# Five load buffers for the first mixer's weight blocks, loads ahead of the modulation chunks, query weights loaded late

## The reference

```python
sh1, sc1, g1, sh2, sc2, g2 = [m[:, None, :] for m in ada(c, ada_w[i], ada_b[i])]
h_l = rmsnorm(x, norm1_g[i]) * (1 + sc1) + sh1
p_lat = h_lat @ w_in
p_ctx = h_ctx @ w_in
q = (rmsnorm(cq, q_norm_g) @ w_uq).reshape(B, T, MLA_HEADS, QK_HEAD_DIM)
kv = (rmsnorm(ckv, kv_norm_g) @ w_ukv).reshape(B, T, MLA_HEADS, QK_NOPE_DIM + V_HEAD_DIM)
```

## Time and profile before

| | |
|---|---|
| median of 3 runs | 1814.38 us (1810.35 to 1815.94) |
| profiled execution | 1805.72 us |
| its span | 1803.9 us |
| mean granted clock of TensorE | 0.962 |
| TensorE busy | 1657.5 us, 92% |
| VectorE, ScalarE, GpSimd busy | 755.1, 435.7, 119.7 us |
| moved by DMA | 586.61 MB, mean 325 GB/s |
| first mixer's blocks 0 to 17 | 38.5 to 113.5 us |

### The profile page before, as it was taken

How to read it: one execution, slowest core, us unless ns; L and a number is a source line. 1 busy time by engine, 2 the same in 40 slices (tenths; PEclk the granted TensorE clock), 3 DMA queues, 4 the chain that set the end, 5 groups by cost and what they waited for, 6 DMA issues and landing times.

```text
span 1803.9 us, 21857 instructions
## 1 busy us (share of the span) xinstructions
PE 1657.5 (92%) x8294; PEld 993.8 (55%) x8294; DVE 755.1 (42%) x1187; ACT 435.7 (24%) x643; POOL 119.7 (7%) x151
## 2 busy tenths in 40 slices
PE   5899899999889999999999999999968897899776
PEld 2763588888678888876433433344423342344222
DVE  5566578787368787654211221222201120112022
ACT  3434554443354444353000000000000000000001
POOL 1752010000410000020000000000000000000000
PEclk8998999999999999999999999999988999899888
DMA  9623559885449887607999999999999999999995
GB/s 353 233 99 117 183 189 340 312 299 192 171 159 330 314 306 270 245 24 302 375 419 421 421 421 421 421 421 422 421 422 421 421 421 421 421 412 421 422 421 204
DMA packets 100430, 586.61 MB, mean 325 GB/s; under 512 B 12048, under 2 KB 13328, under 8 KB 44976
## 3 DMA queue, kind: packets, MB, share of 16 engines
q1 hardware_dynamic: 100336, 585.35, 82.1%
HBM read 584.26 MB, written 1.05 MB: 324 GB/s over the span
## 4 chain that ended last, share of the span: by engine, by line
PE 78%; DMA 11%; DVE 5%; SPq 4%; issue 1%; ACT 1%; DVEq 0%; ACTq 0%
PE psum L1244 23%; PE psum L1260 11%; PE psum L912 4%; PE psum L913 4%; PE psum L914 4%; SPq L421 3%; PE psum L1220 3%; DMA mraw<-gu_dram 3%; PE psum L1029 3%; PE psum L1273 3%; PE psum L933 2%; PE psum L935 2%; PE psum L934 2%; DMA araw<-ada_dram 2%; PE psum L729 2%; PE psum L731 2%
## 5 line engine op out<-in xcount | busy, mean ns | idle before, releaser
L1244 PE MATMUL psum<-mraw,xsat 128*64 128x512 f32 (+2 forms) x1640 | 411.3, 647 | 55.2 <-DMA mraw<-gu_dram 40.9
L1244 PEld LDWEIGHTS psum<-mraw,xsat 128*64 128x64 f32 (+2 forms) x1640 | 135.6, 144 | 305.7 <-issue 304.6
L1260 PE MATMUL psum<-mraw,xsat 128*64 128x512 f32 (+2 forms) x856 | 205.9, 621 | 17.1 <-DMA mraw<-dn_dram 9.9
L912 PE MATMUL psum<-wh,ah 128*128 128x512 f32 x352 | 139.6, 397 | 2.6 <-DVE al L1917 1.8
L1260 PEld LDWEIGHTS psum<-mraw,xsat 128*64 128x64 f32 (+2 forms) x856 | 68.2, 140 | 133.2 <-issue 131.1
L913 PE MATMUL psum<-wl,ah 128*128 128x512 f32 x352 | 137.3, 390 | 0.0
L914 PE MATMUL psum<-wh,al 128*128 128x512 f32 x352 | 137.3, 390 | 0.0
L1803 POOL TENSOR_TENSOR wl<-raw,wh 128x256 fp32r<-128x256 f32 x132 | 108.6, 858 | 396.1 <-DVE work L1944 219.9
L2455 DVE TENSOR_TENSOR oacc<-psum,oacc 128x512 f32<-128x512 f32 x60 | 38.6, 686 | 220.3 <-PE psum L1273 220.3
L1244 PE MATMUL psum<-mlast,xsat 128*64 128x512 f32 (+2 forms) x408 | 118.2, 627 | 0.0
L1965 DVE TENSOR_TENSOR wl<-raw,wh 128x1024 fp32r<-128x1024 f32 x88 | 103.6, 1219 | 33.1 <-ACT wh L1525 33.1
(11 more groups left out here) (374 smaller groups left out, 2423.7 us busy)
## 6 DMA issues: line engine op xcount, KB each, us to landing
mraw<-gu_dram SPq DMA_DIRECT2D x205, 1024.0 KB, 19.2
mraw<-dn_dram SPq DMA_DIRECT2D x107, 1024.0 KB, 25.6
araw<-ada_dram SPq DMA_DIRECT2D x128, 512.0 KB, 4.9
mlast<-gu_dram SPq DMA_DIRECT2D x51, 1024.0 KB, 20.2
raw<-ffa_dram SPq DMA_DIRECT2D x44, 1024.0 KB, 5.1
raw<-ffb_dram SPq DMA_DIRECT2D x44, 512.0 KB, 5.3
mlast<-dn_dram SPq DMA_DIRECT2D x21, 1024.0 KB, 24.2
raw<-blk_dram SPq DMA_DIRECT2D x34, 512.0 KB, 4.8
```

Source lines behind the costliest of these rows:

```text
L912: mm(o, ah3[:, j, tok], wh[:, w], start=(j == 0), stop=False)
L1244: last = mm(ps[4 + n][a * w:(a + 1) * w, :], xs[:, k * P + a * w:k * P + (a + 1) * w], slots[slot][:, i * 2 * D + n * 512:i * 2 * D + (n + ...
L1260: last = mm(ps[n][a * w:(a + 1) * w, :], at[:, k * P + a * w:k * P + (a + 1) * w], slots[slot][:, i * D + n * 512:i * D + (n + 1) * 512], ...
```

## The change

It moves nothing on TensorE, VectorE, ScalarE and GpSimd; the order of their instructions stays. It changes three things.

1. Blocks 3 to 17 rotate over five buffers (`NFIRST_RAW`), the fourth and fifth at columns 3072 and 4096 of `raw`, where the query weights were. Load b waits for cast and subtraction b - 5 for b below 18. The semaphores of the two added buffers are reused from the pairs (`s_afirst[1:3]`), so `RAW_LOADED` gives the count that cast b waits for.
2. In the queue blocks 3 and 4 come ahead of chunks 16 and 17, behind a wait for the third pair product, since the pair lies in these columns. Blocks 7 to 10 come in one piece, and from then on block 9 + n comes ahead of chunk 16 + n, where before chunk 16 + n came ahead of block 6 + n.
3. The query weights are loaded behind block 17, after subtraction 14; `q_product` waits for them by a semaphore of their own (`s_uq`). `uk` and `cone` wait for the fourth pair product only.

The diff, without its hunks of line numbers:

```diff
...
 B_2 = B_Q2
 B_OUT2 = 48
 NB = 56
-NRAW = 3
+NRAW, NFIRST_RAW = 3, 5
 PIECE = 256
 SPLIT = [b % 6 for b in range(B_O)] + [0, 1, 4, 5, 2, 3, 4, 5] * 2
 SPLIT_BEFORE = [max([k + 1 for k in range(b) if SPLIT[k] == SPLIT[b]], default=0) for b in range(B_2)]
-RAW = [(5120 if b >= B_O + NRAW else 0) + (b % NRAW) * D for b in range(B_2)]
+RAW_SLOT = [b % NFIRST_RAW if b < B_O else (b - B_O) % NRAW for b in range(B_2)]
+RAW_LOADED = [16 * (RAW_SLOT[:b + 1].count(RAW_SLOT[b]) + (RAW_SLOT[b] >= NRAW)) for b in range(B_2)]
+RAW = [(5120 if b >= B_O + NRAW else 0) + RAW_SLOT[b] * D for b in range(B_2)]
 MIX_SLOT = (0, 1, 2, 5, 3, 6, 4, 7, 1, 2, 5)
-MIX_BASE = [16 * len(range(i, B_2, NRAW)) for i in range(NRAW)] + [16 * (1 + NF), 16 * (1 + NF), 0, 16 * (1 + NF), 16 * (1 + NF)]
+MIX_BASE = [16 * RAW_SLOT.count(i) for i in range(NRAW)] + [16 * (1 + NF), 16 * (1 + NF), 0, 16 * (1 + NF), 16 * (1 + NF)]
 MIX_LOADED = [MIX_BASE[s] + 16 * MIX_SLOT[:k + 1].count(s) for k, s in enumerate(MIX_SLOT)]
 OUT_BANK = (4, 5, 6, 7, 0, 1, 2, 4)
 
...
         s_con, s_vec, s_xin, s_out = [sem(n) for n in ("consts_loaded", "vectors_loaded", "x_and_ctx_loaded", "out_stored")]
 
         s_par = sem("parameters_loaded")
-        MLA_IN, DFT_IN, LRU_IN, EXP_IN = 48, 64, 64 + 256, 64 + 256 + 48
+        MLA_IN, DFT_IN, LRU_IN, EXP_IN = 32, 48, 48 + 256, 48 + 256 + 48
+
         s_raw = [sem(f"block_loaded{i}") for i in range(NRAW)]
         s_hi, s_lo, s_blk, s_ev = [sem(n) for n in ("block_hi", "block_lo", "block_product", "block_evacuated")]
         s_araw = [sem(f"ada_loaded{i}") for i in range(2)]
         s_afirst = [sem(f"ada_pair_loaded{k}") for k in range(NFIRST - 4)]
+        s_raw, s_uq = s_raw + s_afirst[1:3], s_afirst[0]
         s_ada, s_adp, s_arow, s_acol, s_mod = [sem(n) for n in (
             "ada_acc", "ada_product", "ada_rows", "ada_columns", "mod_ready")]
         s_x = sem("x_chunk")
...
         s_v1, s_v1c, s_f2, s_f2h, s_f2l = [sem(n) for n in (
             "dft_features", "dft_features_copied", "dft_tokens", "dft_hi", "dft_lo")]
         s_th, s_lruo = sem("lru_tanh"), sem("lru_out")
-        s_mix = s_raw + [s_fraw[0], s_fbraw[0], sem("mixer_blocks_loaded"), s_fraw[1], s_fbraw[1]]
+        s_mix = s_raw[0:NRAW] + [s_fraw[0], s_fbraw[0], sem("mixer_blocks_loaded"), s_fraw[1], s_fbraw[1]]
         s_xc = sem("xr_xg_copied")
         s_zero = sem("pads_cleared")
         s_xcv, s_rg1, s_sgm, s_lru, s_mul2, s_sq2, s_gel, s_gelt = [sem(n) for n in (
...
                 sp.dma_start(afirst[k], src.rearrange("(a p) n -> p a n", a=2)).then_inc(s_afirst[k], 16)
 
             def blk(b):
-                if b >= NRAW:
-                    sp.wait_ge(s_hi, b - NRAW + 1)
-                    sp.wait_ge(s_lo, b - NRAW + 1)
-                sp.dma_start(raw[:, RAW[b]:RAW[b] + D], blk_d[b]).then_inc(s_raw[b % NRAW], 16)
+                if b >= NFIRST_RAW:
+                    before = b - (NFIRST_RAW if b < B_O else NRAW)
+                    sp.wait_ge(s_hi, before + 1)
+                    sp.wait_ge(s_lo, before + 1)
+                sp.dma_start(raw[:, RAW[b]:RAW[b] + D], blk_d[b]).then_inc(s_raw[RAW_SLOT[b]], 16)
 
             def expert_load(i, number=None):
                 p, (kind, u, c), a, slot, before = LOADS[i]
...
             for b in range(NRAW):
                 blk(b)
 
+            sp.wait_ge(s_adp, 3)
+            for b in range(NRAW, NFIRST_RAW):
+                blk(b)
             ada(ADA_FIRST)
             ada(ADA_FIRST + 1)
-            for b in range(NRAW, 6):
+            for b in range(NFIRST_RAW, 7):
                 blk(b)
-            sp.wait_ge(s_adp, 8)
-            sp.dma_start(uq, uq_d).then_inc(s_par, 16)
+            sp.wait_ge(s_adp, 4)
             sp.dma_start(uk, uk_d).then_inc(s_par, 16)
             sp.dma_start(cone[:, :], cone_d).then_inc(s_par, 16)
-            blk(6)
-            blk(7)
+            for b in range(7, 11):
+                blk(b)
             for n in range(2, 8):
+                blk(9 + n)
                 ada(ADA_FIRST + n)
-                blk(6 + n)
-            for b in range(14, B_O + 3):
+            blk(17)
+            sp.wait_ge(s_lo, 15)
+            sp.dma_start(uq, uq_d).then_inc(s_uq, 16)
+            for b in range(B_O, B_O + NRAW):
                 blk(b)
             ada(24)
             ada(25)
...
                 last.then_inc(s_qk, 1)
 
             def q_product(j):
+                pe.wait_ge(s_uq, 32)
                 pe.wait_ge(s_qkc, 2 + j)
                 for h in (2 * j, 2 * j + 1):
                     for k in range(3):
...
                 act.wait_ge(s_act, chain[0])
 
             def block_hi(b):
-                act.wait_ge(s_raw[b % NRAW], 16 * (b // NRAW + 1))
+                act.wait_ge(s_raw[RAW_SLOT[b]], RAW_LOADED[b])
                 wait(act, s_blk, SPLIT_BEFORE[b])
                 A(wh[:, SPLIT[b] * D:(SPLIT[b] + 1) * D], raw[:, RAW[b]:RAW[b] + D], ACT.Copy).then_inc(s_hi, 1)
 
```

## The result

| | median of the runs | profiled execution | its span |
|---|---|---|---|
| before | 1812.37 us (1809.02 to 1815.94, 4 runs) | 1805.72 us | 1803.9 us |
| changed | 1799.04 us (1797.89 to 1801.81, 4 runs) | 1801.81 us | 1800.0 us |

The ratio is 0.9928, with a 95% interval of 0.9903 to 0.9954: faster by 13.1 us, between 8.3 and 17.6. The two profiled executions, on the other hand, differ by only 3.9 us. Both discrepancies have to be explained.

What follows compares the result with a forecast made beforehand. It took TensorE's wait in the first mixer for squares behind block 13's late load as the bound; 6.47 + 0.97 + 0.60 = 8.04 us, so 1814.4 - 8.0 = 1806.4 us, range 1801 to 1813.

Steps and rivals of the forecast that it cites:

- The gap and its cause: First mixer, TensorE idle from 83 to 89 us: block 13's load, queued behind chunk 23, delays the squares its sums need.
- The order does it: Sync queue: block 13 was not late through its buffer; its load stood behind a modulation chunk.
- Point 1, standing still: First mixer: TensorE stands still from 82.75 to 89.22, 6.47 us, between block 10 and the sums.
- Points 2 and 3: Lower clock after the idle stretch: the sums' four passes lose 0.97 us, the first matmul behind them 0.60 us.
- The follow-up from cast 6 to block 17: First mixer reckoned in the new order: load 13 issued about 64.9, squares ready near 76.5, subtraction 17 at 97.6.
- Carried to the end at full size: Behind the first mixer all is released by semaphores and own loads, so the 8.0 us reach the kernel's end.
- B, a loss further on: Rival, chance 0.14: later stages' waits or clock take back 5 to 8 us, giving 1811 to 1815.
- the level from which the 8.0 were taken: Starting time of the forecast for the whole kernel: the median of three runs, 1814.38 us.
- A, GpSimd becomes the bound: Rival, chance 0.10: GpSimd's subtractions from block 11 on hold TensorE, 0.7 us lost, a gain of 7.3.
- C: Rival, chance 0.04: slower, 1820, chunk 23 held behind load 16 and thus behind subtraction 11 ending later than 82.1.
- D: Rival, chance 0.04: something unseen holds the squares; half the gap left, a gain of 4, 1810.
- The chances: Whole kernel: faster by over 5.4 us 0.66, slower 0.05, between 0.29; the forecast itself 0.68.

Runs made afterwards that it cites:

- order_only: The kernel before, three buffers, with the block load put ahead of the chunk in the loop over chunks 18 to 23; ratio 0.9972, 5.1 us off.
- late13: The changed kernel with the loads of block 13 and those behind it put back behind chunk 23; ratio to the kernel before 0.999, 1.8 us off.
- before_again: An unchanged copy of the kernel before, run for a second trace; ratio to the kernel before 1.0007 (0.9992 to 1.0021).
- gap_filled: The kernel before with 12 idle TensorE products put behind block 10, ahead of the sums that wait; ratio 0.9975, 4.5 us off.
- opening_late: The changed kernel with loads 3 and 4 and chunks 16 and 17 waiting for the eighth pair product, not the third; ratio to the kernel before 0.9938.
- opening_filled: The changed kernel with 4 idle products in the opening's waits and 6 behind the second row columns; ratio to the kernel before 0.9942.
- uq_later: The changed kernel with the query weights' load moved behind the loads of blocks 18 to 20; ratio to the kernel before 0.9943.

## Why the prediction was wrong in size and right in place

- **The gap and its cause: right.** A late load behind a chunk, shown from both sides by `order_only` and `late13`.
- **The order does it: right, and more than was said.** The prediction gave the two buffers no share of their own. They are worth nothing alone. What is left behind the single exchange is 1.7 us of the stage, and whether it takes the buffers or only a place further ahead wasn't tested.
- **Point 1, standing still, 6.47 us: right.** 6.50 in `before_again`, 6.33 at the least.
- **Points 2 and 3, the clock, 1.57 us: too small by 0.4 to 0.5 in the mean.** The step took one execution for the kernel. Over five traces gap and clock together cost 8.5 us and not 8.04. The split was off too: without the gap the four passes take 1.32 us (83.36 to 84.68) and the first matmul behind them 0.52 (to 85.20), not 1.82 and 0.12. In the trace of the prediction the clock thus cost 1.47 and 0.20, 1.67 together. `gap_filled` gives the clock's part as 1.9.
- **The follow-up from cast 6 to block 17: right.** Load 13 at 66.2 (64.9 reckoned), squares at 76.6 (76.5), subtraction 17 at 98.7 (97.6), the stage from block 10's end 22.59 us (22.70). L1462 began at 86.70, where it was reckoned to be over. L668 came at 105.96 and not 105.45, as block 10 ended 0.6 us later. One reading was wrong without harm: L1442 at 71.27 stood behind cast 10, not only behind TensorE's sums, and came at 69.79.
- **Carried to the end at full size: held, with scatter.** At 748 us, by the same instruction of VectorE, the three traces of the changed kernel are 6.6 to 6.9 us ahead of the first trace of before, and the mean of the three traces of before is 2.1 us behind it: 8.8 us between the kernels. B, a loss further on, was not seen.
- **The step that failed: the level from which the 8.0 were taken.** The prediction saw that the profiled execution lay 8.7 us below the median of three, gave that median a scatter of 2 to 4 us, and still set forecast and lower bound from the three runs (1814.38 - 8, 1810.35 - 8). Later runs of the kernel before put it at 1811 to 1812.4; 1811.5 - 8.5 = 1803.0 would have been the forecast, and the changed kernel's medians of six are 1802.3 and 1802.5. The forecast of 1806.4 was 7.3 us too high: 2.9 are this level, 0.4 points 2 and 3, and by 4.0 the four runs of the changed kernel lie below 1803.0. Its twelve later runs have a median of 1802.5, so 3.4 of these 4.0 are peculiar to the four runs; why they were low isn't known. The range had no room below for a median of few runs on either side. That the 13.1 us are 8.5 plus such scatter is argued, not shown: 8.5 us is a ratio of 0.9953, which the intervals of all three comparisons include.
- **A, GpSimd becomes the bound: no.** It did work without a pause for twelve blocks, which is why the rival was fair, but had over 4 us in hand at the end. A piece of blocks 1 to 17 took 872 to 874 ns in the mean in the three traces of the changed kernel and 812 to 847 in those of before. The Trainium skill names contention with VectorE's two-input instructions (GPSIMD Engine Reference, Key points); the traces agree in the direction, and that it is the cause of these 25 to 60 ns isn't shown.
- **C and D: no.** Subtraction 11 was over at 75.5, far from 82.1. Chunk 23 goes at 83.12, 1.0 us later than before; block 10 ends 0.6 us later too.
- **The chances.** Faster by over 5.4 us was given 0.66; nine tenths of 0.68 and a third of 0.10 make 0.65.

What stays open: whether the change brings some 2 us beyond the 8.5. The three comparisons give 13.1, 9.8 and 10.9 us, and the three variants that keep load 13 early (`opening_late`, `opening_filled`, `uq_later`) 11.2, 10.5 and 10.3: all six, some against the same runs of the kernel before, are above 8.5, and none excludes it. The six spans with an early load 13 average 1799.7 us and the five with a late one 1809.7, that is 10.1 us, 1.6 more than the stage shows; but the first group is spread over 7.3 us and the second over 9.7. By the same instructions of VectorE the groups are 0.4 us apart at 80 us, ahead of the gap, 8.9 at 120, 9.9 at 748 and 10.1 at the end, so that the rest isn't in one place. These runs don't settle it.

## What to carry to other kernels

In a hand-written transfer queue, look for the load that stands behind a transfer whose wait has nothing to do with it; two more buffers brought nothing here while it stood there. When it has moved, look again: behind the first exchange load 13 stood 5 us behind the next chunk, though its buffer was free. When following such a load, look for small work queued behind its consumer in program order: here no matmul of block 13 was late, but the squares behind cast 13 were. And don't take one profile, or a median of three, for the level of a kernel whose clock falls differently in every execution.

## What was not expected of the hardware

The clock of TensorE falls at different moments of the same program. In the opening the granted clock fell between 30 and 36 us (in `opening_filled` at 41) and, that trace apart, stayed low for 10.2 to 17.1 us, over three traces of one kernel 10.2, 10.2 and 13.7. One idle stretch of 6.3 to 6.5 us cost between 1.7 and 2.5 us more than its length (30.74 to 31.53 us less 22.6, less the stretch). The expert stage's beginning cost 3 us more in 10 of 13 traces than in the other three. Single executions of the unchanged kernel are spread over 1805.7 to 1818.6 us, more than the gain of the change. The clock is a part of that: over 76 later executions of it the time falls as the mean granted clock rises, with a correlation of -0.64. The rest isn't explained.
